# The two mixers of a hybrid block, written out as one sequence per engine

## The chip, the core and the metric

The kernel runs on one core of a Trainium2 chip. The metric is the time on the device in microseconds (us), of which the median of several runs is taken. TensorE (PE) multiplies, VectorE (DVE) and ScalarE (ACT) do elementwise work, GpSimd (POOL) a few small things, and SyncE (SP) starts the loads.

## The reference

The input is 256 tokens of width 1024. A first block (two layers) is followed by a second block (two layers); the change is in the second. `swiglu`, the projections and the norms stay as they are.

```python
for l in range(DEPTH):                                   # DEPTH = 2
    x = x + 0.5 * swiglu(rms_norm_2(x, ffn1_norm[l]), ffn1_gate[l], ffn1_up[l], ffn1_down[l])
    h = rms_norm_2(x, mix_norm[l]) @ w_in[l]
...
    y_pool = pool_mixer(u_pool, pool_w[l], pool_scale[l])        # windows 2, 4, 8, 16
    y_moba = moba_attention(qm, km, vm)                          # 4 heads of 64, causal here
    y_dil = dilated_attention(qd, kd, vd)                        # 4 heads of 64, causal, dilations 1, 4, 16
    y_conv = conv_module(u_conv, conv_w[l], conv_b[l], conv_ln_g[l], conv_ln_b[l])   # 31 taps
    mix = jnp.concatenate([y_pool, y_moba, y_dil, y_conv], axis=-1)
    x = x + mix @ w_out[l]
    x = x + 0.5 * swiglu(rms_norm_2(x, ffn2_norm[l]), ffn2_gate[l], ffn2_up[l], ffn2_down[l])
```

With 256 tokens both attentions are a softmax over a table of added logits (`biasc`), and half of that table, the keys after a query, is masked.

## The kernel before

All weights are cut into chunks of 128 x 2048 numbers (1 MB), which one list puts in order (`plan`, L99). SyncE loads a chunk into one of five slots of `raw` as soon as the chunk five places earlier is used up. ScalarE rounds it to `whi` (L733, four slots), VectorE writes the remainder to `wlo` (L1320): this pair of steps is the split. TensorE then multiplies each chunk in 48 products of 128 x 256 (weights high by activations high, high by low, low by high), all of them recorded on L994, the line of the helper `mm`.

The activations lie feature-major: 128 features on the partitions, 256 tokens along them. In the mixer of one layer there are nine chunks of projections (cg and ca for the convolution, qm, km, qd, kd for the queries and keys, up, vm, vd token-major for the pool and the values) and four output chunks wo. Each projection fills one of four banks `accM`; VectorE or ScalarE takes it out before the bank is used again. Queries and keys are rotated: VectorE scales the product twice (L1544, L1545), TensorE multiplies by a rotation matrix (`rot`), VectorE adds (L1627).

There are eight heads, in the steps `scores` (two products of a 64-row query by key), bias and maximum on VectorE (L1642, L1645), exponent on ScalarE (L914), `turn` (four transposes, L1181), a copy on ScalarE (L920), `mix` (the turned weights by the values, token-major), division by the row sum on VectorE (L1678, L1681), `back` (transposes to feature-major, L1208), and the high and low parts (L940, L1697). The convolution is 31 taps of two instructions on VectorE (L1705, L1707), followed by statistics over features (`cstats`) and a normalisation (`cspread`), whose results are the last quarter of the wo product.

What sets the order: `plan` gives each step a chunk position, and sorts the steps of one position by kind. Each engine goes through the chunks. TensorE spreads the steps of a position evenly over the eight parts of that chunk's product, unless the chunk needs one of them first. VectorE does what it takes out of a finished product, then some steps, then the split of the chunk three ahead, then the others; the taps go in six parts of five or six. Three lines set this:

```python
for n in range(TAP_PARTS):
    at(base + 2 + n, "taps", l, n)
for pos in sorted(todo):
    steps.setdefault(min(pos, base + 12), []).extend(sorted(todo[pos], key=lambda s: order[s[0]]))
```

## Time and profile before

| | us |
|---|---|
| median of 3 runs | 2279.4 |
| lowest, highest | 2274.05, 2287.24 |
| the profiled execution | 2291.71 |
| its span, first to last instruction | 2289.9 |
| TensorE busy | 2166.0 |
| VectorE busy | 1439.4 |
| ScalarE busy | 1006.9 |

The page gives the busy time of each engine; matmuls overlap, so a busy TensorE may still be slow. The stretches tell how many instructions fell into a part of the span and which clock TensorE was granted there (1.00 is full speed). In the chain of waits each step is followed back to what released it, so the distance of two starts is what an instruction costs on the path. In the order of time, a bracket behind a row says how long the engine had been idle and for whom.

### The profile page before, as it was taken

What the parts mean: (1) busy time and instruction counts of PE and PEld (TensorE: products, weight loads), DVE (VectorE), ACT (ScalarE), POOL (GpSimd) and SP (SyncE); (2) the same over time, 40 slices, a digit from 0 to 9 for tenths busy, and PEclk for the clock granted to TensorE, in tenths of its full rate; (3) what the DMA queues carried; (4) which work ended last, traced back from release to release, by engine and by line L of the source; (5) the groups of instructions that cost most, each with busy time, mean ns of one, the idle gap of its engine ahead of it and who ended that gap; (6) DMA issues with size and microseconds to landing.
All of it is one profiled execution on the core that took longest, in us unless ns stands there. A gap on an engine that the chain in (4) does not pass through costs nothing.

```text
span 2289.9 us, 39444 instructions
## 1 busy us (share of the span) xinstructions
PE 2166.0 (95%) x17460; PEld 2108.3 (92%) x17460; DVE 1439.4 (63%) x1701; ACT 1006.9 (44%) x1166; POOL 49.1 (2%) x58
## 2 busy tenths in 40 slices
PE   7999999899899999989997999879999999879998
PEld 7999999899889999989997999769999999769997
DVE  6565564666665556457675756856656656855664
ACT  5554354444455444444444443334444434333442
POOL 1000000000000000000000000000000000000000
PEclk8999999999999999999998999889999999979999
DMA  5444543355344455445552555314555554313552
GB/s 198 163 149 172 182 181 140 137 184 186 134 155 172 150 184 184 148 142 186 189 190 99 184 185 184 111 56 156 196 192 183 181 189 176 129 56 130 185 186 90
DMA packets 52858, 366.08 MB, mean 160 GB/s; under 512 B 5904, under 2 KB 5904, under 8 KB 9296
## 3 DMA queue, kind: packets, MB, share of 16 engines
q1 hardware_dynamic: 52272, 361.21, 43.9%
q8 instruction: 138, 2.26, 0.4%
q0 software_dynamic: 416, 2.35, 0.3%
q14 instruction: 32, 0.26, 0.0%
HBM read 362.49 MB, written 1.05 MB: 159 GB/s over the span
## 4 chain that ended last, share of the span: by engine, by line
PE 75%; DVE 10%; issue 10%; ACT 4%; DMA 1%; POOL 1%; POOLq 0%; ACTq 0%; DVEq 0%
PE accM L994 43%; PE scoreP L994 16%; PE outP L994 8%; PE turnP L994 7%; DVE wlo L1320 3%; DVE yc L1707 1%; ACT whi L733 1%; PE turnP L1181 1%; ACT ew L914 1%; ACT xh L746 1%; PE outP L1208 0%; DMA raw<-in_W 0%; ACT sq L752 0%; DVE cen L1398 0%; DVE cen L1404 0%
## 5 line engine op out<-in xcount | busy, mean ns | idle before, releaser
L1320 DVE TENSOR_TENSOR wlo<-raw,whi 128x2048 fp32r<-128x2048 f32 x336 | 768.5, 2290 | 417.4 <-ACT whi L733 416.1
L733 ACT ACTIVATE whi<-raw 128x2048 fp32r<-128x2048 f32 x336 | 638.5, 1908 | 240.9 <-PE accM L994 139.9
L994 PE MATMUL accM<-xh,whi 128*128 128x256 f32 x1152 | 339.2, 294 | 11.2 <-DVE xl L1418 10.4
L994 PE MATMUL scoreP<-xh,whi 128*128 128x256 f32 x1152 | 328.3, 285 | 13.9 <-DVE xl L1418 9.4
L994 PE MATMUL scoreP<-xl,whi 128*128 128x256 f32 x1152 | 326.2, 283 | 0.0
L994 PE MATMUL scoreP<-xh,wlo 128*128 128x256 f32 x1152 | 326.1, 283 | 0.0
L994 PE MATMUL accM<-xl,whi 128*128 128x256 f32 x1152 | 325.6, 283 | 0.0
L994 PE MATMUL accM<-xh,wlo 128*128 128x256 f32 x1152 | 325.3, 282 | 0.0
L994 PE MATMUL accM<-fh,whi 128*128 128x256 f32 x1056 | 296.8, 281 | 4.1 <-DVE wlo L1320 4.1
L994 PE MATMUL accM<-fl,whi 128*128 128x256 f32 x1056 | 296.5, 281 | 0.0
L994 PE MATMUL accM<-fh,wlo 128*128 128x256 f32 x1056 | 296.5, 281 | 0.0
L994 PEld LDWEIGHTS accM<-xh,whi 128*128 128x128 f32 x1152 | 220.8, 192 | 21.8 <-issue 21.6
L994 PEld LDWEIGHTS scoreP<-xh,whi 128*128 128x128 f32 x1152 | 221.5, 192 | 14.9 <-issue 14.3
L994 PEld LDWEIGHTS accM<-xl,whi 128*128 128x128 f32 x1152 | 220.6, 192 | 2.7 <-issue 2.5
L994 PEld LDWEIGHTS accM<-xh,wlo 128*128 128x128 f32 x1152 | 222.3, 193 | 0.0
L994 PEld LDWEIGHTS scoreP<-xh,wlo 128*128 128x128 f32 x1152 | 221.2, 192 | 0.0
L994 PEld LDWEIGHTS scoreP<-xl,whi 128*128 128x128 f32 x1152 | 220.8, 192 | 0.2
L994 PEld LDWEIGHTS accM<-fh,whi 128*128 128x128 f32 x1056 | 200.0, 189 | 4.8 <-DVE wlo L1320 4.8
L994 PEld LDWEIGHTS accM<-fh,wlo 128*128 128x128 f32 x1056 | 200.0, 189 | 0.0
L994 PEld LDWEIGHTS accM<-fl,whi 128*128 128x128 f32 x1056 | 199.2, 189 | 0.0
L994 PE MATMUL turnP<-xl,whi 128*128 128x256 f32 x480 | 134.5, 280 | 0.0
L994 PE MATMUL turnP<-xh,wlo 128*128 128x256 f32 x480 | 134.5, 280 | 0.0
(263 smaller groups left out, 4256.3 us busy)
## 6 DMA issues: line engine op xcount, KB each, us to landing
raw<-in_W SPq DMA_DIRECT2D x336, 1024.0 KB, 4.8
biasr<-in_bias SPq DMA_DIRECT2D x16, 256.0 KB, 2.7
raw<-in_memT SPq DMA_DIRECT2D x2, 1024.0 KB, 5.4
cc<-in_consts POOLq DMA_DIRECT2D x1, 1536.0 KB, 7.1
x<-in_xT SPq DMA_DIRECT2D x4, 256.0 KB, 4.3
out<-x SPq DMA_DIRECT2D x4, 256.0 KB, 2.5
c<-in_consts SPq DMA_DIRECT2D x1, 464.5 KB, 6.2
par<-in_par POOLq DMA_DIRECT2D x2, 203.5 KB, 3.6
```

The source lines that it names most:

```text
L733: nc.scalar.activation(whi[:, hi_slot(c), :], raw[:, raw_slot(c), :], ACT.Copy).then_inc(split_hi.sem, 1)
L746: ins = nc.scalar.activation(xh[:, k, :], x[:, k, :], ACT.Copy, scale=gain(n, k))
L914: ins = nc.scalar.activation(ew[:, e0 + i, :], src, ACT.Exp, bias=negmax[:, e0 + i:e0 + i + 1], scale=scale, accum_out=rsum[:, s0 + i:s0 + ...
L994: return nc.tensor.matmul(dst, a, b, start=start, stop=stop, skip_group_check=True)
L1181: ins = nc.tensor.transpose(turnP[:, k * S + t * P:k * S + (t + 1) * P], src[t][:, k * P:(k + 1) * P], ident)
L1320: v.tensor_tensor(wlo[:, raw_slot(c), :], raw[:, raw_slot(c), :], whi[:, hi_slot(c), :].bitcast(F32), ALU.subtract).then_inc(split_lo.sem, 1)
L1707: ins = v.scalar_tensor_tensor(yc[:, m, :], src, w, yc[:, m, :], ALU.mult, ALU.add)
```

## The change

The nine projections and four wo chunks no longer take their steps from the plan. For each mixer, every engine now has one written-out function `mixer(l)`, which lists products in eighths, taps one by one, splits and head steps. `product` takes a range of its eight parts (k0, k1). The wo chunks come in the order 1, 0, 2, 3, where it was 0, 1, 3, 2. Banks are named in a table. The norm ahead of the mixer is cut in pieces (`norm_front`, `norm_var`, `norm_diag`), with splits between them.

The heads change in form. Scores, bias, maximum and exponent leave out the block of keys 128 to 255 for queries 0 to 127, which is masked: 384 columns stand where 512 stood. The division by the row sum is done on the exponents before the turn (`even`). `weigh` takes the values as the stationary side, so that the result comes out feature-major in 64 rows, two heads in one bank; `otok` and the `back` transposes go. The order of the other stages is unchanged.

```diff
+MIXER_BANKS = {"cg": "acc0", "ca": "acc1", "qm": "acc2", "qm turned": "acc0", "km": "acc3", "km turned": "acc1",
+               "qd": "acc2", "qd turned": "acc3", "kd": "acc0", "kd turned": "acc1", "up": "acc1", "vm": "acc2",
+               "heads 0": "acc2", "heads 1": "acc1", "vd": "acc0", "heads 2": "out", "heads 3": "out"}
...
-            for r, k in (("cg", "F"), ("ca", "F"), ("qm", "F"), ("km", "F"), ("qd", "F"), ("kd", "F"),
-                         ("up", "T"), ("vm", "T"), ("vd", "T")):
-                c = add(k, r, l)
-                if r in ("qm", "km", "qd", "kd"):
-                    at(c + 2, "rot", chunks[c])
-                if r == "up":
-                    at(c + 2, "pool", chunks[c])
-                    at(c + 2, "poolw", chunks[c])
...
-            for j in (0, 1, 3, 2):
+            for j in (1, 0, 2, 3):
...
-            for n in range(TAP_PARTS):
-                at(base + 2 + n, "taps", l, n)
...
+            def exponent(l, i):
+                act.wait_ge(mix_maxed.sem, mix_maxed.at((l, i)))
+                if i >= 2:
+                    act.wait_ge(mix_turned.sem, mix_turned.at((l, i - 2)))
+                for t in range(2):
+                    e, s0 = 2 * (i % 2) + t, 2 * (i % 4) + t
+                    ins = nc.scalar.activation(ew[:, e, keys(t)], logits(i)[:, tri(t)], ACT.Exp,
+                                               bias=negmax[:, e:e + 1], accum_out=rsum[:, s0:s0 + 1])
+                ins.then_inc(mix_expd.sem, 1)
+
+            def keep_turned(l, i):
+                act.wait_ge(mix_turned.sem, mix_turned.at((l, i)))
+                if i >= 2:
+                    act.wait_ge(mix_weighed.sem, mix_weighed.at((l, i - 2)))
+                nc.scalar.activation(turned_heads(i)[:, 0:TRI], turnP[:, 0:TRI], ACT.Copy)\
+                    .then_inc(mix_turn_kept.sem, 1)
+
+            def heads_hi(l, pair):
+                act.wait_ge(mix_weighed.sem, mix_weighed.at((l, 2 * pair + 1)))
+                nc.scalar.activation(zh[:, 2 + pair, :], mixer_bank(f"heads {pair}")[:, 0:S], ACT.Copy)\
+                    .then_inc(mix_hi.sem, 1)
...
+                move_tokens(m["up"])
+                keep_turned(l, 1)
+                keep_pool(l)
+                pool_hi(l)
+                move_tokens(m["vm"])
+                exponent(l, 2)
+                split_next(m["wo2"])
+                exponent(l, 3)
+                heads_hi(l, 0)
+                keep_turned(l, 2)
...
-            def product(c, hooks):
+            def product(c, hooks, k0=0, k1=KT):
...
+            def rotate(c):
+                l, r = c["l"], c["role"]
+                bank[MIXER_BANKS[r + " turned"]].claim(pe, mix_roped, (l, r))
+                pe.wait_ge(mix_took.sem, mix_took.at((l, r)))
+                mm(mixer_bank(r + " turned"), con("rot2"), rraw[:, (r[0] == "k") * 1, :], True)\
+                    .then_inc(mix_rotated.sem, 1)
...
+            def turn(l, i):
+                turnB.claim(pe, mix_turn_kept, (l, i))
+                pe.wait_ge(mix_evened.sem, mix_evened.at((l, i)))
+                for t in range(2):
+                    for k in range(t + 1):
+                        ins = nc.tensor.transpose(turnP[:, (k + t) * P:(k + t + 1) * P],
+                                                  ew[:, 2 * (i % 2) + t, k * P:(k + 1) * P], ident)
+                ins.then_inc(mix_turned.sem, 1)
+
+            def weigh(l, i):
+                kind, j, pair = kind_of(i), i % 4, i // 2
+                if i % 2 == 0:
+                    bank[MIXER_BANKS[f"heads {pair}"]].claim(pe, mix_lo, (l, pair))
+                pe.wait_ge(mix_turn_kept.sem, mix_turn_kept.at((l, i)))
+                pe.wait_ge(mix_moved.sem, mix_moved.at((l, "v" + kind)))
+                v0 = 64 * j + (S if kind == "d" else 0)
+                o = mixer_bank(f"heads {pair}")[64 * (j % 2):64 * (j % 2) + 64, :]
+                e = turned_heads(i)
+                mm(o[:, 0:S], v2[:, 0, v0:v0 + 64], e[:, 0:S], True, False)
+                mm(o[:, P:S], v2[:, 1, v0:v0 + 64], e[:, S:TRI], False, True).then_inc(mix_weighed.sem, 1)
...
+                product(m["cg"], {})
+                product(m["ca"], {}, 0, 3)
+                norm_stats(n)
+                product(m["ca"], {}, 3, 8)
+                product(m["qm"], {}, 0, 4)
+                norm_spread(n)
+                product(m["qm"], {}, 4, 8)
+                product(m["km"], {}, 0, 3)
+                rotate(m["qm"])
...
+                product(m["vm"], {}, 7, 8)
+                rotate(m["kd"])
+                product(m["vd"], {}, 0, 1)
+                weigh(l, 0)
+                product(m["vd"], {}, 1, 2)
+                weigh(l, 1)
...
+                product(m["wo0"], {}, 5, 8)
+                conv_stats(l)
+                turn(l, 4)
+                turn(l, 5)
+                weigh(l, 4)
+                turn(l, 6)
+                weigh(l, 5)
+                turn(l, 7)
+                weigh(l, 6)
+                weigh(l, 7)
+                conv_spread(l)
+                product(m["wo2"], {})
+                product(m["wo3"], {})
...
+            def root_scaled(c):
+                r = c["role"]
+                dve.wait_ge(used.sem, used.at(c["c"]))
+                cos, sin = (csr[:, i, :].unsqueeze(1).broadcast_to([P, 2, S]) for i in range(2))
+                rr = rraw[:, (r[0] == "k") * 1, :].rearrange("p (m s) -> p m s", m=2)
+                v.tensor_tensor(rr, pair_of(c), sin, ALU.mult)
+                v.tensor_tensor(turned_to(c), pair_of(c), cos, ALU.mult).then_inc(mix_took.sem, 1)
+
+            def rotated_sum(c):
+                l, r = c["l"], c["role"]
+                dve.wait_ge(mix_took.sem, mix_took.at((l, r)))
+                dve.wait_ge(mix_rotated.sem, mix_rotated.at((l, r)))
+                v.tensor_tensor(turned_to(c), mixer_bank(r + " turned").rearrange("p (m s) -> p m s", m=2),
+                                turned_to(c), ALU.add).then_inc(mix_roped.sem, 1)
+
+            def add_bias(l, i):
+                dve.wait_ge(mix_scored.sem, mix_scored.at((l, i)))
+                if i >= 2:
+                    dve.wait_ge(mix_expd.sem, mix_expd.at((l, i - 2)))
+                v.scalar_tensor_tensor(logits(i)[:, 0:TRI], scoreP[:, i % 2, 0:TRI], 0.125,
+                                       biasc[:, (kind_of(i) == "d") * 1, :], ALU.mult, ALU.add)\
+                    .then_inc(mix_biased.sem, 1)
+
+            def maximum(l, i):
+                dve.wait_ge(mix_biased.sem, mix_biased.at((l, i)))
+                for t in range(2):
+                    e = 2 * (i % 2) + t
+                    ins = v.tensor_reduce(negmax[:, e:e + 1], logits(i)[:, tri(t)], AX, ALU.max, negate=True)
+                ins.then_inc(mix_maxed.sem, 1)
+
+            def even(l, i):
+                dve.wait_ge(mix_expd.sem, mix_expd.at((l, i)))
+                s, s0 = mrs[:, 10 + 2 * (i % 2):12 + 2 * (i % 2)], 2 * (i % 4)
+                link(v.reciprocal(s, rsum[:, s0:s0 + 2]))
+                for t in range(2):
+                    e = ew[:, 2 * (i % 2) + t, keys(t)]
+                    ins = v.tensor_scalar(e, e, s[:, t:t + 1], None, ALU.mult)
+                ins.then_inc(mix_evened.sem, 1)
...
+            def heads_lo(l, pair):
+                dve.wait_ge(mix_hi.sem, mix_hi.at((l, pair)))
+                v.tensor_tensor(zl[:, 2 + pair, :], mixer_bank(f"heads {pair}")[:, 0:S],
+                                zh[:, 2 + pair, :].bitcast(F32), ALU.subtract).then_inc(mix_lo.sem, 1)
...
+                split_next(m["qm"])
+                split_next(m["km"])
+                norm_var(n)
+                split_next(m["qd"])
+                norm_diag(n)
+                split_next(m["kd"])
+                keep_spread(n)
+                gate_scaled(m["cg"])
+                scale_tables()
+                root_scaled(m["qm"])
+                conv_scaled(m["ca"])
+                conv_gated(l)
+                split_next(m["up"])
+                taps(l, 0, 1)
+                rotated_sum(m["qm"])
...
+                taps(l, 30, 31)
+                add_bias(l, 6)
+                even(l, 4)
+                add_bias(l, 7)
+                maximum(l, 6)
+                even(l, 5)
+                maximum(l, 7)
+                conv_var(l)
+                even(l, 6)
+                split_next(m["wo2"])
+                even(l, 7)
+                heads_lo(l, 2)
+                conv_diag(l)
+                split_next(m["wo3"])
+                heads_lo(l, 3)
+                split_next(m["sg0"])
+                conv_centre(l)
+                split_next(m["su0"])
+                conv_act(l)
+                conv_lo(l)
```

The order that results, in two places. VectorE in the first mixer, amid the taps, before: yc is the convolution's sum, wlo a split, rraw, q2 and k2 belong to the rotation.

```order
L1320 TENSOR_TENSOR wlo<-raw,whi 128x2048
L1707 SCALAR_TENSOR_TENSOR yc<-hpad,par,yc 128x256 x10
L1544 TENSOR_TENSOR rraw<-accM,angle 128x512
L1545 TENSOR_TENSOR k2<-accM,angle 128x512
L1627 TENSOR_TENSOR q2<-accM,q2 128x512
L1320 TENSOR_TENSOR wlo<-raw,whi 128x2048
L1707 SCALAR_TENSOR_TENSOR yc<-hpad,par,yc 128x256 x10
L1544 TENSOR_TENSOR rraw<-accM,angle 128x512
L1545 TENSOR_TENSOR q2<-accM,angle 128x512
L1627 TENSOR_TENSOR k2<-accM,k2 128x512
```

And after, a little later in the taps: negmax and logit are maximum and bias, ew the exponents.

```order
L1812 SCALAR_TENSOR_TENSOR yc<-hpad,par,yc 128x256 x2
L1845 TENSOR_REDUCE negmax<-logit 128x1 x2
L1812 SCALAR_TENSOR_TENSOR yc<-hpad,par,yc 128x256 x2
L1845 TENSOR_REDUCE negmax<-logit 128x1 x2
L1812 SCALAR_TENSOR_TENSOR yc<-hpad,par,yc 128x256 x2
L1837 SCALAR_TENSOR_TENSOR logit<-scoreP,cc 128x384
L1812 SCALAR_TENSOR_TENSOR yc<-hpad,par,yc 128x256 x2
L1851 RECIPROCAL mrs<-rsum 128x2
L1854 TENSOR_SCALAR ew<-ew,mrs 128x128
L1854 TENSOR_SCALAR ew<-ew,mrs 128x256
L1812 SCALAR_TENSOR_TENSOR yc<-hpad,par,yc 128x256 x2
L1851 RECIPROCAL mrs<-rsum 128x2
```

Five taps in a row became single taps, each followed by one step of a head, of a rotation or by a split.

TensorE where the last heads are done, before: outP takes the convolution's spread, a transpose and a head, and accM the products of a wo chunk.

```order
L994 MATMUL accM<-zh,wlo 128x256
L994 MATMUL accM<-zh,whi 128x256
L994 MATMUL accM<-zl,whi 128x256
L994 MATMUL accM<-zh,wlo 128x256
L994 MATMUL outP<-diag,ones 128x128 x4
L1208 MATMUL outP<-c0,otok 128x128 x2
L994 MATMUL outP<-v2,eT 128x64 x4
L994 MATMUL accM<-zh,whi 128x256
L994 MATMUL accM<-zl,whi 128x256
L994 MATMUL accM<-zh,wlo 128x256
```

And after, behind the chunk wo0:

```order
L1331 MATMUL turnP<-c0,ew 128x128 x6
L1098 MATMUL outP<-eT,v2 64x256
L1098 MATMUL outP<-eT,v2 64x128
L1331 MATMUL turnP<-c0,ew 128x128 x3
L1098 MATMUL outP<-eT,v2 64x256
L1098 MATMUL outP<-eT,v2 64x128
L1331 MATMUL turnP<-c0,ew 128x128 x3
L1098 MATMUL outP<-eT,v2 64x256
L1098 MATMUL outP<-eT,v2 64x128
L1098 MATMUL outP<-eT,v2 64x256
L1098 MATMUL outP<-eT,v2 64x128
L1098 MATMUL outP<-diag,ones 128x128 x4
```

The turns and weighings of the last four heads, which stood a few at a time between parts of wo chunks, now stand in one row, between wo0 and wo2.

## Rows read from the trace of the kernel before

**Rows 1.** the page, busy time by engine: us, share of the span, instructions

```profile
PE 2166.0 (95%) x17460; PEld 2108.3 (92%) x17460; DVE 1439.4 (63%) x1701; ACT 1006.9 (44%) x1166; POOL 49.1 (2%) x58
```

**Rows 2.** busy time by stretch: from:to, length, then busy us (instructions), granted clock, DMA

```profile
1406.00:1563.00 157.00, 131.79 (x918) 119.10 (x918) 106.94 (x185) 56.53 (x92) 1.38 (x2) 0.89 0.28 101
...
1926.00:2083.00 157.00, 130.65 (x895) 118.53 (x894) 104.22 (x179) 54.51 (x88) 1.38 (x2) 0.87 0.28 101
```

**Rows 3.** tile accM on PE, first mixer: ns min/median/max, first and last start

```profile
L994 PE MATMUL accM<-xh,whi x96: 275/277/1202, 1417.6 to 1462.2; 128*128 128x256 f32 x96
...
L994 PE MATMUL accM<-zh,wlo x64: 275/280/416, 1515.7 to 1563.1; 128*128 128x256 f32 x64
```

**Rows 4.** the same for the second mixer

```profile
L994 PE MATMUL accM<-xh,whi x96: 275/281/1202, 1938.2 to 1983.2; 128*128 128x256 f32 x96
...
L994 PE MATMUL accM<-zh,wlo x64: 276/280/416, 2033.7 to 2085.6; 128*128 128x256 f32 x64
```

**Rows 5.** chain of waits, in a feed-forward stage: start, us, work

```profile
1259.48 11.31 PE scoreP L994 x96
```

**Rows 6.** chain of waits inside the first mixer

```profile
1447.27 0.60 DVE q L1545
1447.87 2.20 DVE wlo L1320
...
1500.89 0.44 PE turnP L1181 x4
1501.33 0.71 PE accM L994 x6
...
1503.38 1.06 PE scoreP L994 x4
1504.43 0.90 PE accM L994 x6
...
1552.75 0.84 PE outP L994 x8
```

**Rows 7.** DVE in order of time, first mixer: start, us, line, work

```profile
1449.98 4.55 DVE L1707 SCALAR_TENSOR_TENSOR yc<-hpad,par,yc 128x256 f32<-128x256 f32 x10
...
1512.87 0.42 DVE L1428 TENSOR_TENSOR diag<-outP,c 128x256 f32<-128x256 f32 x1
...
1516.91 0.42 DVE L1697 TENSOR_TENSOR zl<-outP,zh 128x256 fp32r<-128x256 f32 x1
```

**Rows 8.** costliest groups, first mixer, shapes apart: busy us, mean ns, idle before

```profile
L1642 DVE SCALAR_TENSOR_TENSOR logit<-scoreP,cc 128x512 f32<-128x512 f32 x8 | 5.5, 688 | 11.8 <-PE scoreP L994 11.8
L1645 DVE TENSOR_REDUCE negmax<-logit 128x2 f32<-128x512 f32 x8 | 5.5, 686 | 0.3
...
L994 PE MATMUL outP<-cc,up 128*64 128x256 f32 x16 | 2.5, 463 | 0.0
```

**Rows 9.** tile ew on DVE, whole program: ns min/median/max

```profile
L1658 DVE TENSOR_SCALAR ew<-ew,mrs x16: 347/352/356, 53.5 to 696.6; 128x256 f32<-128x256 f32 x16
```

**Rows 10.** PE in order of time, first mixer, two rotations

```profile
1448.02 2.04 PE L994 MATMUL accM<-rraw,c 128*128 128x512 f32 x2 [5.51 <-DVE q L1545]
...
1456.11 1.10 PE L994 MATMUL accM<-rraw,c 128*128 128x512 f32 x2
```

**Rows 11.** DVE in order of time, first mixer, a late head

```profile
1527.08 0.69 DVE L1642 SCALAR_TENSOR_TENSOR logit<-scoreP,cc 128x512 f32<-128x512 f32 x1 [5.05 <-PE scoreP L994]
```

**Rows 12.** three-us stretches of the first mixer, columns as in rows 2

```profile
1448.00:1451.00 3.00, 2.98 (x8) 1.97 (x9) 2.96 (x4) 0.00 (x0) 0.00 (x0) 0.51 0.00 0
...
1484.00:1487.00 3.00, 3.00 (x9) 1.94 (x9) 2.90 (x7) 0.00 (x0) 0.00 (x0) 0.50 0.03 8
...
1514.00:1517.00 3.00, 1.82 (x11) 1.82 (x12) 2.02 (x11) 1.34 (x2) 0.69 (x1) 0.80 0.00 0
...
1541.00:1544.00 3.00, 3.00 (x20) 3.00 (x20) 0.30 (x2) 0.00 (x0) 0.00 (x0) 0.65 0.00 0
...
1547.00:1550.00 3.00, 3.00 (x28) 3.00 (x27) 0.42 (x1) 1.54 (x3) 0.00 (x0) 1.00 0.13 22
```

More of the change, by code:

```diff
@@ L812, in take @@
                 if "ends" in c:
+                    if c["role"] == "sd" and c["f"] == 0:
+                        norm(c["ends"])
+                        return True
                     norm(c["ends"], lambda: split_at(pos + 2),
@@ L1248, in _ @@
+            PE_STEPS = ("rot", "back", "mix", "turn", "scores")
             SPREAD = 8
@@ L1305, in _ @@
             v = nc.vector
-            BEFORE_SPLIT = ("scores", "rot", "back",
-                            "mix", "turn", "yc", "lam", "cstats", "cspread", "pool", "poolw")
+            BEFORE_SPLIT = ("scores", "rot", "back", "mix", "turn", "yc", "lam")
             def split(c):
@@ new lines, in taps @@
+            def taps(l, i0, i1):
+                for i in range(i0, i1):
+                    for m in range(2):
+                        src, w = tap(i, m)
+                        if i == 0:
+                            ins = v.tensor_scalar(yc[:, m, :], src, w, col("conv_b", m, 1, P2), ALU.mult, ALU.add)
+                        else:
+                            ins = v.scalar_tensor_tensor(yc[:, m, :], src, w, yc[:, m, :], ALU.mult, ALU.add)
+                    if i < TAPS - 1:
+                        link(ins)
+                    else:
+                        ins.then_inc(tapped.sem, 1)
```

627 lines of the change are left out of this document (399 added, 228 removed).

## The prediction

> **What bounds the kernel now.** I read the page first: TensorE is busy 2166 of 2289.9 us [rows 1], so outside its gaps nothing but matmul work sets the time. Then the stretches: the two in which the mixers lie have the low granted clocks, 0.89 and 0.87, and only 918 and 895 matmuls in 157 us [rows 2], where a feed-forward stage puts 96 products into 11.31 us [rows 5]. A chunk of 48 matmuls therefore costs 5.65 us, 0.118 us each. The change touches the two mixers alone, so everything else stays.
>
> A mixer begins with the first product of chunk cg and ends with the last product of the last wo chunk. The first runs from 1417.6 to 1563.2 [rows 3], the second from 1938.2 to 2085.7 [rows 4]: 145.6 and 147.5 us, mean 146.5. Its 13 chunks are 13 x 5.65 = 73.5 us of TensorE. So some 73 us of each mixer are head steps, waits and half clock. Three views say which. TensorE waits 5.51 us for VectorE, which is still in its taps when qm's product needs scaling [rows 10]. VectorE waits in turn for TensorE's scores, 11.8 us in sum, 5.05 us once at the end [rows 8, 11]. And behind each longer gap stands a granted clock of 0.50, the lower of the two levels (1.2 GHz against 2.4) [rows 12]: the rotation that waited took 2.04 us and the later one, at full clock, 1.10 [rows 10]. Engines take turns here; none is busy throughout (VectorE 107 of 157 us).
>
> **VectorE in the changed mixer.** The order is now one list, so I sum it. Distances from start to start in the chain of waits are what an instruction costs in a row: a split 2.20 us, an operation over 512 columns 0.60 [rows 6]. Ten tap instructions take 4.55 us, so one tap (two instructions) 0.915 with its hand-over [rows 7].
> - 13 splits (qm to su0): 28.6.
> - 31 taps: 28.4, as before, only cut finer; each piece already waits for its own chain.
> - 20 operations of 512 columns (gate, tables, four times two scalings and a sum, two for the convolution's input, four at its end): 12.2.
> - Bias: 384 columns where 512 cost 688 ns [rows 8]. Between 0.60 in a row and 0.42, what 256 columns take [rows 7], I take 0.50; eight: 4.0.
> - Maximum: one instruction of 686 ns [rows 8] becomes two of 128 and 256 columns. Bounds 0.42 (one of 256) and 0.84; I take 0.62; eight: 5.0.
> - Normalising now before the turn: a reciprocal and two scalings of ew, 128 and 256 columns; 256 cost 0.352 in the same form [rows 9]. I take 0.80 (bounds 0.55 and 0.95); eight: 6.4. The old normalisation, on 64 columns twice, goes.
> - Statistics, diagonals, low parts: the convolution's are 4.0 us from 1512.87 to 1516.91, with a 0.8 us visit to GpSimd that the new order covers [rows 7]; with the norm's and the five small ones 7.3.
>
> Together 92 us, against 107 of busy time in the old window, which holds other stages too [rows 2]. The first split starts 7.2 us after cg, as today (the norm before it is unchanged).
>
> **TensorE in the changed mixer.** 13 chunks, 73.5. Scores: 1.06 for 512 columns [rows 6]; 384 bring 0.80, and I add 0.15 because the six products behind scores took 0.90 and not 0.71 [rows 6]: eight, 7.6. Turns: three transposes where four took 0.44 [rows 6]: with the return 0.5, eight, 4.0. Weighing: today's mix is 0.84 for four products per tile pair [rows 6]. The new one streams 384 columns onto 64 output rows; scaled from the scores that is 0.80. Bounds 0.64 and 1.06; I take 0.95 with the return: 7.6. The four `back` transposes go, and with them VectorE's way through otok; I count nothing for them, only their waits. Rotations 4 x 1.05 = 4.2. Pool 2.5 [rows 8]; its second half and the statistics, unchanged, about 6.6. Sum 106 us. So both engines are nearly full, and the mixer cannot be shorter than about 106.
>
> At one place a rule speaks against the change. After scores on 64 rows, products come back 0.19 us late (0.90 for 0.71), after transposes they do not [rows 6]. The Trainium skill's page TensorEngine Tiling (Key Properties) says that changing the tiling mode drains TensorE, and by that rule the new weighing, on 64 columns, pays at both of its ends where today's mix on 128 pays nothing: 16 x 0.19 = 3.0 us a mixer, 1.8 more than the 8 x 0.15 in my sum.
>
> **Do they fit together?** I walk both lists with these durations, t counted from cg's first product. Five VectorE splits and the norm go ahead of the first tap, which starts at t = 22. TensorE has only 1 us of gap by then: the norm's statistics sit inside ca, the spread inside qm, and qm is scaled (t = 20) before km ends (t = 26), so the 5.51 us gap is gone. The banks are free each time (qd in acc2 at 26, kd in acc0 at 33). TensorE ends kd at 42, vm at 59.5. Here VectorE waits: exponent(2) stands on ScalarE behind `keep_pool`, `pool_hi` and `move_tokens(vm)`, and ends at about 61.5, where VectorE wants it at 59 for even(2): 2.6 us. heads_lo(1) waits for vd's last head, 2.0. The convolution's statistics cost 0.8 (TensorE ends wo0 at 86 and the statistics at 88), small ones 0.6. So VectorE ends at 7.2 + 92 + 6 = 105.5 with conv_lo. wo2 starts at 98, behind heads_lo(3), and ends at 104; wo3 needs conv_lo, so the mixer ends at 105.5 + 5.65 = 111 us. What is late last is VectorE's list, no longer a round trip.
>
> **The clock.** I add 2 us. Between t = 86 and 98 TensorE has some 7 us of small steps in 12; at 1514 such a stretch fell to 0.80 [rows 12]. If wo2 starts at half clock it costs at most 5 us more, of which the wait for conv_lo covers 2. The Trainium skill (TensorE: Matmul & The Clock Gate, "Why this matters for your kernels") advises against idle gaps between bursts, as the clock drops after them; by that rule the old gaps of 5.51 us would be throttled, and the trace agrees [rows 10, 12].
>
> Hence 113.5 us a mixer against 146.5: 33 saved each, 66 in both. The profiled execution took 2291.7 us (span 2289.9 and 1.8 around it) and gives 2225.7; it was 12.3 above the median of the runs shown, and nothing in the mixers makes that difference, so from the median 2279.4 I come to **2213.4 us**.
>
> **Rivals.**
> - A, the forecast: the lists mesh, mixers of 107 to 119 us, as the small terms go to their bounds; savings of 55 to 79 us give 2200 to 2224. Chance 0.64.
> - B, the clock stays low for longer: the list puts 16 small fp32 steps with waits into vm and vd, where half clock lasted from about 1484 [rows 12]. Each 10 us of TensorE's full-clock work done at half clock is 10 us more, since TensorE has only 5 us of slack; one or two such pieces give mixers of 119 to 132, 2224 to 2250. For it: the clock falls after gaps. Against: by the walk no gap above 2.6 us is left. Chance 0.17.
> - C, nearly no waits: TensorE's own 106 us and smaller steps, mixers of 100 to 107, 2186 to 2200. Against it: three waits that I can name. Chance 0.10.
> - D, an interlock: strict lists let no engine go past a late step, so a single step put too early (rotate(kd), weigh(2) or exponent(2)) holds a whole list, 8 to 12 us, each mixer. Two such holds give 2250 to 2270. Chance 0.04.
> - E, slower: half clock through the head stage and the tail. TensorE's 106 us would need 146.5 - 111 = 35 us of them at half clock just to lose the gain, a third of its work; at half of the work (53 us) a mixer takes 164 and the kernel 2314. For it: the old mixer had twelve of these 3-us stretches, 36 us, at 0.66 or less, the first at 1448 and the last at 1541 [rows 12]. Against: those followed gaps that the new order closes. Chance 0.05, 0.02 of it within the bound of no change.
>
> **How the numbers follow.** The likeliest case gives 2213. The range must leave out 2 in 10 at most: from 2194 (all of A and 0.04 of C's 0.10) to 2243 (0.13 of B's 0.17), which holds 0.81. A measurement of this kernel can tell 0.5%, 11 us, from no change: faster by more is A, B, C and D, 0.95; within 0.5% 0.02; slower 0.03.
>
> **What would show it.** Right: from cg's first product to wo3's last some 113 us in both mixers; granted clock over that stretch above 0.95; VectorE over 90% busy from the first tap to conv_lo; wo3's first product released by the low part of the convolution (zl, 512 columns). Wrong: a gap of TensorE over 3 us before vd; stretches at 0.50 during vm, vd or wo1; a weighing step over 1.1 us at full clock; ScalarE's exponents waited for by more than 3 us. Each mixer at 125 us would mean B, and stretches outside the mixers that differ by over 5 us would mean that I overlooked an edit.

## The result

The changed kernel takes 2202.4 us (median of 4 runs, 2196.8 to 2202.7) where the kernel before took 2278.0 on the same chip (4 runs, 2274.1 to 2287.2): ratio 0.966, 95% interval 0.962 to 0.969, 75.6 us less. The forecast was 2213.4 in a range of 2194 to 2243. The mixers' part came out larger than forecast, and one sentence of the reasoning does not hold for most of the mixer: which engine is late.

The changed kernel's page, busy time by engine as in [rows 1]:

```profile
PE 2117.2 (96%) x17364; PEld 2059.8 (94%) x17364; DVE 1432.3 (65%) x1717; ACT 1003.6 (46%) x1166; POOL 53.1 (2%) x58
```

TensorE's busy time fell by 48.8 us with 96 instructions fewer; 33.8 of that lie in the two mixers, and the last section says where the rest may come from. VectorE's and ScalarE's hardly moved, so the gain is not work taken off those two. A mixer is read from the first product of cg to the last of the last wo chunk. For the first one (tile accM on PE: ns min/median/max, first and last start), as in [rows 3]:

```profile
L1098 PE MATMUL accM<-xh,whi x96: 276/281/682, 1403.8 to 1445.4; 128*128 128x256 f32 x96
...
L1098 PE MATMUL accM<-zh,wlo x64: 276/279/280, 1474.5 to 1512.5; 128*128 128x256 f32 x64
```

And the busy times of just those two stretches (columns as in [rows 2]), first of the kernel before, then of the changed one:

```profile
1417.60:1563.10 145.50, 120.29 (x821) 107.60 (x820) 98.44 (x173) 51.27 (x85) 1.38 (x2) 0.88 0.26 95
1938.20:2085.60 147.40, 121.87 (x820) 109.93 (x821) 97.58 (x172) 50.27 (x82) 1.38 (x2) 0.86 0.26 93
```

```profile
1403.80:1512.60 108.80, 102.81 (x774) 91.44 (x773) 95.21 (x182) 49.78 (x86) 3.35 (x2) 1.00 0.35 127
1886.80:1997.00 110.20, 105.53 (x774) 93.23 (x773) 95.40 (x182) 49.83 (x86) 3.35 (x2) 0.95 0.34 125
```

146.5 us became 109.5, 37.0 in each mixer. The account for the first: TensorE stood for 25.2 us (145.5 - 120.3) and stands for 6.0. Of its 120.3 busy us some 13.5 were the extra time of the half clock: in each 3-us stretch the busy time times one minus the granted clock, summed over the mixer. At full clock its work was 106.8 us and is 102.8. So 36.7 = 19.2 less standing + 13.5 less half clock + 4.0 less work. This is a book of where the time lay; what caused what is the experiments' matter.

The two mixers give 74.0 and the medians 75.6, which agree. The two profiled executions differ by 89.0 (2291.71 and 2202.72): the first mixer began 13.8 us earlier in the changed kernel's, ahead of any changed instruction. The last section says what that is.

TensorE's waits in the first mixer of the changed kernel (engine, what it was to do, line, for whom: us in all, times, longest):

```profile
PE turnP L1331 <- ACT eT L1015: 2.2, 2, 1.5
PE outP L1098 <- DVE zl L1859: 1.8, 1, 1.8
PE accM L1098 <- DVE zl L1895: 1.0, 1, 1.0
PE turnP L1331 <- DVE ew L1854: 0.7, 1, 0.7
```

All of them lie behind 1489.2, in the last fifth of the mixer. Until then TensorE has no gap above 0.2 us in 85 us. In the second mixer, and in both of the control below, it has one more, of 0.7 us, for the norm's diagonals at t = 16 (t counts from the mixer's first product). The 5.51 us ahead of the rotation [rows 10] and the 5.05 us for which VectorE waited on a late head's scores [rows 11] are gone.

### The profile page after: what moved, and what is told of

It is laid out like the page before. It is cut to its first block, busy times and chain, and to the rows that moved or that the text cites. A ratio compares the mean times of both kernels' runs of the same rounds, so it can differ in the third digit from the quotient of the medians.

```text
span 2200.9 us, 39332 instructions
## 1 busy us (share of the span) xinstructions
PE 2117.2 (96%) x17364; PEld 2059.8 (94%) x17364; DVE 1432.3 (65%) x1717; ACT 1003.6 (46%) x1166; POOL 53.1 (2%) x58
## 4 chain that ended last, share of the span: by engine, by line
PE 80%; issue 9%; DVE 7%; ACT 3%; POOL 1%; DMA 0%; POOLq 0%; ACTq 0%; DVEq 0%
PE accM L1098 48%; PE scoreP L1098 16%; PE outP L1098 7%; PE turnP L1098 7%; DVE wlo L1531 2%; ACT whi L747 1%; PE turnP L1278 1%; ACT xh L765 1%; ACT ew L926 1%; ACT x L812 0%; POOL small L689 0%; PE outP L1304 0%; ACT sq L771 0%; DVE cen L1625 0%; DVE mrs L2064 0%
## 5 line engine op out<-in xcount | busy, mean ns | idle before, releaser
L1098 PE MATMUL turnP<-xh,whi 128*128 128x256 f32 x480 | 133.4, 278 | 0.0
```

The source lines that it names most:

```text
L1098: return nc.tensor.matmul(dst, a, b, start=start, stop=stop, skip_group_check=True)
```

## The experiments

Twelve kernels, each timed in five rounds beside the kernel before, whose median was 2274.1, 2274.7 and 2275.0 in the three sessions. "Mixers" is read in each profile as above. The changed kernel itself, run once more (control_after), is what the others are compared with; it ran in the first session only, so the eight kernels of the later two are compared across chips. Its profile has both mixers undisturbed, that is without half clock:

| kernel | median us | ratio to before, 95% | mixers us | each against control |
|---|---|---|---|---|
| control_after | 2201.4 | 0.969, 0.966 to 0.972 | 108.8, 108.7 | |
| taps_in_six | 2218.7 | 0.977, 0.973 to 0.981 | 118.2, 118.0 | +9.4 |
| six_taps_moved | 2212.6 | 0.973, 0.970 to 0.977 | 111.5, 113.9 | +4.0 |
| full_squares | 2208.2 | 0.972, 0.968 to 0.975 | 112.1, 112.4 | +3.5 |
| load_in_body | 2221.1 | 0.976, 0.973 to 0.979 | 118.0, 117.5 | +9.0 |
| load_body_filled | 2211.2 | 0.973, 0.969 to 0.976 | 112.9, 112.8 | +4.1 |
| load_in_tail | 2215.0 | 0.974, 0.971 to 0.977 | 114.5, 114.6 | +5.8 |
| load_at_waits | 2202.3 | 0.970, 0.967 to 0.973 | 109.1, 109.3 | +0.5 |
| tail_reordered | 2193.8 | 0.966, 0.963 to 0.969 | 106.8, 106.7 | -2.0 |
| square_first | 2194.4 | 0.964, 0.960 to 0.967 | 105.3, 105.1 | -3.6 |
| before_filled | 2269.8 | 0.998, 0.996 to 1.001 | 141.8, 143.8 | (-3.7 against before) |
| before_taps_later | 2285.0 | 1.006, 1.003 to 1.008 | 148.0, 149.8 | (+2.5 against before) |

The medians carry some 5 us of scatter from other stages, so a difference of a few us is read from the mixers of one profile of each kernel, and where both speak they agree in sign. A difference under about 1 us in a mixer is not told from nothing: TensorE's busy time on the same work differs by that much between undisturbed mixers (101.9 to 102.9 us).

> The changed kernel once more, unaltered, beside the three that follow, so that all four are compared on one chip. Both theories expect 2202 us or near it, and mixers of 109 to 110 us.

It repeats: 2201.4 against 2202.4, mixers of 108.8 and 108.7.

**Which part of the change paid: the placing of the taps.** The 31 taps go back into six blocks:

```diff
-                taps(l, 24, 25)
-                pool_lo(l)
-                taps(l, 25, 26)
+                pool_lo(l)
+                taps(l, 25, 31)
                 split_next(m["wo0"])
...
```

> The changed kernel, but with VectorE's 31 taps gathered again into six runs (0-4, 5-9, 10-14, 15-19, 20-24, 25-30), each where its first tap stands now; nothing else is moved. Theory (the order makes the gain, since TensorE no longer waits for VectorE's taps): VectorE reaches its second scaling 2.7 us later, where TensorE has 0.4 us of slack today, and the later runs hold scores and maxima back too; 2 to 6 us more per mixer, with half clock behind the gaps perhaps, so 2206 to 2216 us. Rival (only the projections' start matters, the cut taps do nothing): within 2 us of the control. Second rival (the cut of the taps is the whole gain): mixers of 130 us and more, over 2240 us.

It cost 9.4 us a mixer, more than the 2 to 6 expected. VectorE in order of time, where it hurts (start, us, line, work, idle before and its releaser):

```profile
1474.95 5.45 DVE L1812 SCALAR_TENSOR_TENSOR yc<-hpad,par,yc 128x256 f32<-128x256 f32 x12
1480.32 2.28 DVE L1531 TENSOR_TENSOR wlo<-raw,whi 128x2048 fp32r<-128x2048 f32 x1
...
1491.36 0.56 DVE L1837 SCALAR_TENSOR_TENSOR logit<-scoreP,cc 128x384 f32<-128x384 f32 x1 [4.22 <-PE scoreP L1098]
```

The block of six taps holds up the split of wo0. TensorE runs dry for 2.42 us at 1482.65, works at a granted clock of 0.50 behind it, and VectorE then pays 4.22 us waiting for scores that come late. By the sum used above, the half clock's extra time is 6.6 of the 9.4 us in either mixer, and TensorE stands only 2.9 us longer than in the control, so more of the loss is booked on the clock than on the waits. The next kernel moves that one block behind the maximum of group 5 and changes nothing else:

```diff
-                taps(l, 25, 31)
                 split_next(m["wo0"])
                 add_bias(l, 4)
                 maximum(l, 4)
                 add_bias(l, 5)
                 maximum(l, 5)
+                taps(l, 25, 31)
```

> The version with the taps in six blocks (which was 17 us slower than the changed kernel), with its last block of six taps moved from ahead of the split of wo0 to behind the maximum of score group 5. Same instructions, same six blocks. Theory: what that version lost was one place, the split and the scores of the late heads that waited 5.3 us behind the block while TensorE stood (gaps of 2.4 and a half clock behind them); 3 to 6 us of the 9.3 in each mixer come back, 6 to 12 in all. Rival: it lost by the number of blocks, each of which holds something up a little: under 2 in each mixer comes back. A second rival: the stats of the local branch come later by the block and eat all that is won: no gain or a loss.

5.4 of the 9.4 come back: one place made more than half of the loss. 2.2 of the rest is TensorE's wait for the scaled k, which VectorE does behind the first block of five taps (rotated sum of qm, then the scaling of km), a row in both profiles:

```profile
PE accM L1098 <- DVE k L1824: 2.2, 1, 2.2
```

The second mixer lost 2.4 more than the first, and only there did half clock follow (13.6 us of its stretches). TensorE's wait for k was 2.2 us in both, so a gap of this length may or may not bring the half clock.

**The triangular scores.** Scores, bias, exponents and turns over full squares again (bias 512 columns, four turns, weighing 256 columns each):

```diff
-TRI = P + S
+TRI = 2 * S
...
-                    for k in range(t + 1):
+                    for k in range(2):
```

> The changed kernel with the masked block of keys put back into the heads: scores, bias, maximum, exponent, scaling and turn over 512 columns, four transposes, two products of 256 columns in the weighing; the order is unaltered. Theory (the form of the heads is a small part): TensorE does about 4 us more per mixer and VectorE about 4, both full, so 4 to 6 us per mixer and 2210 to 2215 us. Rival (the smaller heads make the gain): 15 us or more per mixer, over 2232 us.

3.5 us a mixer, a little under the 4 to 6 expected and far from the rival's 15. TensorE's busy time in the first mixer is 105.3 against 102.2, 3.1 us more. VectorE's is longer too, by 2.7 us (bias 1.1, maximum 1.1, scaling of the exponents 0.5). Both engines got nearly the same amount of extra work, so this run prices the triangle but does not say which of them binds.

**Who binds where.** The prediction says that VectorE's list is late last, the trace says that TensorE has no gap until 1489. Seven useless operations of 512 columns go into VectorE's list at two places:

```diff
                 taps(l, 3, 4)
+                load(7)
...
                 conv_diag(l)
+                load(7)
```

> The changed kernel with seven more operations in VectorE's list behind the fourth tap (otok = cs2 * csr, 128x512, each 0.69 us and by the step from start to start 0.61, so 4.3 us in each mixer; nothing reads the result). Theory: until the stats of the local branch TensorE has no gap, it is TensorE's own sum that binds there, and VectorE's waits for others in that stretch (0.6 + 1.2 + 2.2 = 4.0 us in the profile) take the 4.3 in: 0 to 2 us in each mixer, 0 to 4 in all. Rival (what the prediction's text says, that VectorE's list binds all through the mixer): 4 us or more in each, 8 to 10 in all.

> The changed kernel with the same seven operations (4.3 us in each mixer) behind the diagonal of the local branch's stats, that is in the tail. Theory: there VectorE's list is what everything waits for, nothing hides them: 4 to 5 us in each mixer, 8 to 10 in all. Rival: TensorE's sum binds to the end, the tail has slack too: under 2 in each.

The load was larger than reckoned: 5.05 us in the rows, 0.72 each with the hand-over, where 4.3 stood in the expectations. The tail paid all of it, 5.8 us; the 0.7 on top came with some 7 us at half clock in each mixer, most of them inside TensorE's wait. The body missed both expectations: 9.0 us a mixer, nearly twice the load, where 0 to 2 was the theory and 4 or more, 8 to 10 in both mixers together, the rival. Three-us stretches of that kernel's first mixer:

```profile
1434.00:1437.00 3.00, 3.00 (x28) 3.00 (x27) 2.96 (x4) 0.00 (x0) 0.00 (x0) 1.00 0.18 76
1437.00:1440.00 3.00, 1.33 (x12) 1.13 (x10) 2.86 (x5) 1.92 (x1) 0.00 (x0) 1.00 0.64 208
1440.00:1443.00 3.00, 0.41 (x2) 0.44 (x3) 2.90 (x6) 0.00 (x0) 0.00 (x0) 0.55 0.34 142
1443.00:1446.00 3.00, 3.00 (x11) 2.13 (x11) 2.93 (x7) 0.00 (x0) 0.00 (x0) 0.50 0.02 5
1446.00:1449.00 3.00, 3.00 (x11) 2.35 (x11) 2.97 (x4) 0.00 (x0) 0.00 (x0) 0.50 0.00 0
...
1452.00:1455.00 3.00, 3.00 (x25) 2.81 (x24) 2.06 (x6) 0.47 (x1) 0.00 (x0) 1.00 0.00 0
```

```profile
PE scoreP L1098 <- DVE k L1830: 4.3, 1, 4.3
```

The load stands ahead of the rotated sum of km, and TensorE wants k for the first scores just when it is done. So TensorE stood for 4.3 us, and then did 11 matmuls in 3 us where it does 22 to 28 at full clock, until about 1451. My theory read "no gap" as "slack", which it is not. The next kernel divides the 9.0. It fills the gap with idle products, so that only the clock differs:

```diff
                 product(m["kd"], {}, 0, 2)
+                pe.wait_ge(outB.reader[0].sem, outB.reader[0].at(outB.reader[1]))
+                for _ in range(8):
+                    mm(outP[:, 0:S], ones[:, :], con("cos1"), True)
                 scores(l, 0)
```

> The version with seven more VectorE operations behind the fourth tap (which made each mixer 9.0 us longer, for 5.05 us of operations), with eight products of ones by a table of cosines (full float32, 256 columns, some 0.5 us each, 4.1 us in all, result read by nobody) on TensorE ahead of the first scores, where it stood for 4.3 us. Theory: the 9.0 us were 4.3 of standing and then 9 to 12 us in which the same work ran at a granted clock of 0.50; with the gap filled the clock stays, and 3 to 4.5 us in each mixer come back, 6 to 9 in all. Rival: the 9.0 come from the chain of VectorE and ScalarE that the load shifts, whatever the clock: 0 to 1 in each.

```profile
1441.00:1444.00 3.00, 3.00 (x22) 2.82 (x22) 2.86 (x5) 1.92 (x1) 0.00 (x0) 1.00 0.60 169
1444.00:1447.00 3.00, 2.19 (x11) 1.64 (x10) 2.90 (x5) 0.00 (x0) 0.00 (x0) 1.00 0.44 186
1447.00:1450.00 3.00, 3.00 (x18) 2.20 (x19) 2.93 (x7) 0.00 (x0) 0.00 (x0) 1.00 0.00 0
```

With the gap filled the granted clock stays at 1.00 and 4.9 of the 9.0 are gone, a little more than expected, in both mixers nearly alike (5.1 and 4.7). The same VectorE load costs 4.1 without the half clock and 9.0 with it. (In the first mixer of load_in_body the clock fell a second time, in the tail at 1500 to 1510; in the second only behind the gap.) Another kernel puts five such operations where VectorE itself waits:

```diff
+                load(2)
                 even(l, 2)
...
+                load(3)
                 heads_lo(l, 1)
```

> The changed kernel with the same kind of VectorE operations where VectorE itself waits for ScalarE: two ahead of the normalising of head 2 (wait there 1.2 us) and three ahead of the split of head pair 1 (wait 2.2 us); 0.72 us each, 3.6 us in each mixer. Theory (VectorE has slack at these waits and none at the place of the earlier load): 0 to 1 us in each mixer, 0 to 2 in all. Rival (what the prediction says, VectorE's list is what is late all through): 3.6 in each, 7 in all.

```profile
1462.14 1.42 DVE L1999 TENSOR_TENSOR otok<-cs,angle 128x512 f32<-128x512 f32 x2
1463.59 0.17 DVE L1851 RECIPROCAL mrs<-rsum 128x2 f32<-128x2 f32 x1
...
1471.01 2.14 DVE L1999 TENSOR_TENSOR otok<-cs,angle 128x512 f32<-128x512 f32 x3
1473.19 0.42 DVE L1859 TENSOR_TENSOR zl<-accM,zh 128x256 fp32r<-128x256 f32 x1
```

3.6 us of load cost 0.5 us a mixer: both waits (1.19 and 2.17 us in the changed kernel) have vanished from the rows and the load stands in their stead. TensorE's busy time on the same work is 0.5 to 1.0 us above the control's, so the 0.5 may be no cost at all. VectorE's list is thus not late without a break: it has slack of 1 to 2 us at two places in the body, some 0.7 at the rotated sum of km (5.05 of load made a wait of 4.3), and none in the tail. This refutes the rival as it stood, but it is less than a test of the prediction, whose walk had waits of VectorE at just these two places (2.6 and 2.0 us). That TensorE sets the pace of the body rests on its having no gap there. The chain of waits of the changed kernel says the same: it stays on TensorE from the start of the first mixer and passes to VectorE only here (start, us, work):

```profile
1487.63 1.74 PE outP L1098 x8
...
1489.40 0.43 DVE diag L1655
```

**How much of the old loss was the clock.** The same filling in the kernel before, in five of its gaps (n is 10, 4, 6, 3 and 6 products, put in ahead of the step that waits):

```diff
+                for _ in range(n):
+                    mm((outP if to == "out" else turnP)[:, 0:S], ones[:, :], con("cos1"), True)
...
+                fill(name, what)
```

> The kernel before with idle products on TensorE (as above, 256 columns, 0.5 us at full clock) in its gaps, so that the clock has less reason to fall: 10 ahead of the rotation of qm, 4 ahead of qd's, 6 ahead of the turn of head 1, 3 ahead of the local branch's stats and 6 ahead of its spread. Everything else, the order on VectorE too, is as before. In the profile of before TensorE is busy 120.8 us of the first mixer and the mean granted clock there is 0.88, that is some 35 us of 146 at the half clock. Theory A (the waits set the time, the half clock only works inside them): 0 to 3 us less in each mixer. Theory B (the half clock is a price of its own, as the 9.0 us for a load of 5.05 suggest): 5 to 12 us less in each, 10 to 24 in all, and the granted clock of the mixers rises to 0.95 or more.

```profile
1402.30:1544.10 141.80, 124.40 (x879) 112.21 (x878) 98.43 (x174) 51.13 (x84) 1.38 (x2) 0.96 0.28 97
1919.10:2062.90 143.80, 127.35 (x878) 115.45 (x879) 97.54 (x172) 50.20 (x83) 1.38 (x2) 0.94 0.27 96
```

3.7 us a mixer, just above theory A's 3 and below B's 5. By the same sum as above the half clock's extra time fell from 13.5 to 4.2 us in the first mixer, so 9.3 us of clock were won and only 3.7 of time. The other 5.6 or so turned into longer standing, for the engines it waited for were no faster: standing and idle products together are 30.9 us (17.4 + 13.5) where standing was 25.2. In the kernel before, the clock's fall lay mostly inside the waits. In the changed one it depends on the place. In the body it counts nearly in full: by the same sum 4.8 us of half clock in the second mixer of load_in_body, and 4.7 us of time. In the tail, where TensorE waits anyway, a part is covered: 4.2 us in the second mixer of the changed kernel, and 1.4 us of time. The medians (5.1 us, interval of the ratio up to 1.0005) can't prove this gain; the mixers of one profile carry it.

**A part alone in the kernel before.** Each of the six blocks of taps (not three, as the expectation has it), and the square, the stats and the spread behind them, one chunk later:

```diff
-                at(base + 2 + n, "taps", l, n)
-            at(base + 2 + TAP_PARTS, "csquare", l)
-            at(base + 9, "cstats", l)
-            at(base + 10, "cspread", l)
+                at(base + 3 + n, "taps", l, n)
+            at(base + 3 + TAP_PARTS, "csquare", l)
+            at(base + 10, "cstats", l)
+            at(base + 11, "cspread", l)
```

> The kernel before with each of its three blocks of taps, and the square, the stats and the spread of the local branch, one chunk later: one part of the change alone, and in the coarse steps of the kernel before. Theory (one gap closed leaves the others; the block only changes whom it holds up): the 5.5 us gap at the rotation of qm goes or shrinks, and each mixer gains 0 to 5 us, 0 to 10 in all, of the 37 in each that the whole change gave. Rival (the place of the taps is most of what was lost): 10 us or more in each.

Both theories missed, since it is 2.5 us a mixer slower. The gap of 5.51 us ahead of the rotation [rows 10] is gone (the longest such wait in the first mixer is 1.7 now), and two others grew in its stead, from 3.69 and 3.82 us at the same steps (the first mixer again):

```profile
1497.70 1.97 PE L994 MATMUL outP<-v,eT 128*128 128x64 f32 x8 [7.30 <-DVE zl L1697]
...
1535.53 0.66 PE L1208 MATMUL outP<-c,otok 128*128 128x128 f32 x2 [5.45 <-DVE zl L1730]
```

TensorE stands for 30.5 us in that mixer, where it stood for 25.2. The wait of 7.30 is behind a block: VectorE does six taps in one piece (5.46 us from 1491.86) just ahead of the low part that TensorE needs. The wait of 5.45 is behind the spread and its bank, which this edit moved too, so the run does not price the blocks alone. At the two places tried in this kernel, blocks in one piece held somebody up. The cut into pieces that fit between two steps somebody waits for is worth some 9 us of the 37, by taps_in_six; that is its price with everything else of the change in place.

**A better order.** The changed kernel's waits of TensorE lie in the tail, all but the 0.7. This version puts scores and the convolution's stats into wo1 and wo0 earlier, deals wo0's products out between the turns, gives the spread a bank of the scores in place of the heads' bank, covers three waits of VectorE, and moves the split of su0 behind the low part of the convolution:

```diff
-                product(m["wo0"], {}, 5, 8)
+                product(m["wo0"], {}, 0, 3)
                 conv_stats(l)
                 turn(l, 4)
+                product(m["wo0"], {}, 3, 4)
                 turn(l, 5)
+                product(m["wo0"], {}, 4, 6)
                 weigh(l, 4)
...
```

> The changed kernel with its ends meshed anew. TensorE is full up to the end of wo0 there, VectorE from then on. So: scores of the last two heads move into wo1, the convolution's statistics in front of wo0's last five eighths, which then fill the gaps between the last turns and weighings; the convolution's spread goes to a bank of scoreP, so that it doesn't wait for the low part of the last heads; on VectorE three waits are covered (the bias of head 2, the scaling of head 2 and the low part of the second pair each move behind other work) and the split of su0 moves behind the convolution's low part; on ScalarE the exponents 4 and 5 go ahead of a split that waits for wo1. Theory (TensorE is short of its 5.9 us of gaps only at the tail, VectorE has 5 us of waits before it): 3 to 5 us less per mixer, 2192 to 2197 us, TensorE's gaps per mixer under 3 us. Rival (the chain turn, copy, weigh, high part, low part of the last heads binds by its own latency): less than 1 us per mixer, 2200 to 2203 us.

2.0 us a mixer, less than the 3 to 5 expected, and TensorE still stands for 4.7 us and not under 3. Its two longest waits name what is left:

```profile
PE accM L1098 <- DVE zl L1862: 1.5, 1, 1.5
PE outP L1098 <- ACT yc L973: 1.3, 1, 1.3
```

The 1.3 is the stats' wait for the square, which stands on ScalarE behind a split that nobody needs yet:

```diff
-                split_next(m["sg0"])
                 conv_square(l)
+                split_next(m["sg0"])
```

> The version with the reordered tail, and in ScalarE's list the square of the convolution ahead of the split of sg0 in place of behind it. In the profile of the reordered tail TensorE waits 1.3 us for this square, which stands behind a split of 1.8 us. Theory (the tail is one chain and each of its waits counts): 1 to 1.3 us in each mixer, 2 to 3 in all, against the reordered tail. Rival: another chain (the late heads' turns, through ScalarE) ends as late: 0 to 0.5 in each.

1.6 us a mixer more, where 1 to 1.3 was expected, and the row of 1.3 is gone. Together 3.6 us a mixer, 7 in all: 2194 us against 2201. That is 0.3%, less than the medians can tell apart; both mixers of both profiles show it.

## Why the prediction was right, and where it was not

- **What goes.** The round trips and the 5.51 us gap went, as said. The forecast of a mixer was 113.5 us, it took 109.5; 66 saved in both were forecast, 74 measured. Of the 4.0, some 2.4 are VectorE's sum and 1.3 the clock, both below, and 0.3 is a slip: 7.2 + 92 + 6 is 105.2 and not 105.5.
- **The signs named beforehand.** The granted clock was 1.00 and 0.95. VectorE was busy for 71.4 of the 78.2 us from the first tap to conv_lo, 91%. There was no gap of TensorE above 0.7 us before the tail, no stretch at 0.50 before t = 87, no weighing above 0.86 us at full clock, and no wait for exponents above 1.2. These came true.
- **"What is late last is VectorE's list": wrong for four fifths of the mixer.** TensorE has no gap but the 0.7 to t = 85, and load_at_waits shows VectorE with slack on the way. It is right for the tail: wo3's first product is released by the convolution's low part (zl L1895, wait 1.0 to 1.2) in the first mixer and in both of the control, and load_in_tail costs its whole length. The walk had all this in it, both engines near full and VectorE waiting twice. The sentence summed it up wrongly. The forecast did not suffer, as the two engines' sums (106 and 105 us) were so close that either one as the binding engine gives nearly the same time; to that extent the right number is luck and no proof of the sentence.
- **VectorE's sum.** 92 us plus 6 of waits behind a start at 7.2 gave conv_lo at 105.5, and wo3's first product came at t = 103.1. Mis-sized terms: normalising 0.67 for 0.80 (-1.0 in eight), maximum 0.53 for 0.62 (-0.7), the wait for exponent(2) 1.19 for 2.6 (-1.4). Bias 0.48 for 0.50 and the other waits (2.17 for 2.0, 0.74 for 0.8) were right. These three took 3.1 us off and wo3 came 2.4 earlier, so other terms were some 0.7 too small. Rows of the bias and of a normalisation:

```profile
1439.66 0.56 DVE L1837 SCALAR_TENSOR_TENSOR logit<-scoreP,cc 128x384 f32<-128x384 f32 x1
1440.14 0.87 DVE L1812 SCALAR_TENSOR_TENSOR yc<-hpad,par,yc 128x256 f32<-128x256 f32 x2
...
1464.14 0.17 DVE L1851 RECIPROCAL mrs<-rsum 128x2 f32<-128x2 f32 x1 [1.19 <-ACT ew L1007]
1464.35 0.55 DVE L1854 TENSOR_SCALAR ew<-ew,mrs 128x128 f32<-128x128 f32 x2
```

- **TensorE's sum.** 106 us forecast, 102.8 measured at full clock. The terms are costs in the chain of waits with the return to products, so they are read there:

```profile
1437.70 0.85 PE scoreP L1098 x4
1438.55 0.90 PE accM L1098 x6
...
1456.85 1.93 PE outP L1098 x16
...
1468.29 3.07 PE accM L1098 x22
1471.36 0.33 PE turnP L1331 x3
```

A turn of three cost 0.33 for 0.50 (1.4 us in eight) and the pool 1.93 for 2.5 (the row it came from [rows 8] held half clock). Scores cost 0.85 and 0.19 more in the six products behind them, 1.04 for 0.95, which goes the other way by 0.7. Weighing was sized right: the 22 matmuls from 1468.29 are 18 products, 2.12 us at 0.118, and one weighing, which leaves 0.95. The rest of the 3.2 I did not find in single terms.
- **The drain on a change of tiling** (the Trainium skill, TensorEngine Tiling, Key Properties) would have put 1.8 us more into the sum, and the sum was too large without it. The trace of the changed kernel has its price. A weighing and the product behind it:

```profile
1463.79 0.86 PE L1098 MATMUL accM<-eT,v 128*64 128x256 f32 x4
1464.59 0.38 PE L1098 MATMUL accM<-whi,xh 128*128 128x256 f32 x1
```

From start to start a weighing takes 0.80 us, and 0.95 with its return, so the changes of tiling at its two ends cost at most some 0.15 together, less than half of the 0.38 (0.19 at each end) that I priced by the rule. A turn changes no tiling and has 0.08 of the same kind (0.33 against 0.25 from start to start), so how much of the 0.15 is the drain stays open.
- **The clock.** 2 us a mixer were forecast, in the stretch between the late heads and wo2. It fell just there, in the second mixer alone (1976 to 1988) and in neither of the control's, 1.4 us in one mixer of four, although the waits are alike in all four. A three-us stretch of that mixer:

```profile
1979.00:1982.00 3.00, 2.69 (x11) 1.35 (x10) 2.67 (x7) 0.92 (x3) 0.00 (x0) 0.50 0.00 0
```

- **Rival B's price** was right for the body and too high for the tail. It says that TensorE's work at half clock is paid in full once TensorE binds. Load_in_body against load_body_filled shows it in the body (second mixer: 4.7 us of time for 4.8 of half clock). In the tail the second mixer of the changed kernel paid 1.4 for 4.2.
- **Rival D**, an interlock by one step too early or too late, did not happen. Load_in_body and taps_in_six are what it would look like, 9 us a mixer each. Its range is a slip: two holds of 8 to 12 us in each mixer give 2245 to 2261, not 2250 to 2270.
- **"Stretches outside the mixers that differ by over 5 us would mean that I overlooked an edit": wrong as a test.** They differed by 14 us with no edit there. Between the mixers it was 374.2 and 375.0 us, but ahead of them the cadence of the products differed, which is below.

Two shares are measured, each by taking it out of the changed kernel: 9 us for cutting the taps and 3.5 for the triangle. If they add up, the other 24 us of the 37 are the rest of the change as a whole: strict lists, the order of the wo chunks, the norm in pieces and the feature-major heads. No run parts these, so which of them closed the gaps is argued from the trace and not shown.

## What to carry over

An engine without a gap in the trace is the one that binds there, but the engine feeding it can still be on time by a hair. So measure slack by putting a known load into its list at the place in question; at a place where it waits already, the load only fills the wait. Cut a long run of small operations into pieces that fit between the steps others wait for. While it stays in blocks, the place decides: moving one block gave back 5.4 us of 9.4, moving all six by a chunk cost 2.5. And price a gap of TensorE at its length only where something else is late anyway. Where TensorE binds, the half clock behind a gap can cost about the gap once more (4.7 to 5.1 us behind 4.3), but it does not follow each gap: behind waits of 2.2 us it came in one mixer of six_taps_moved and not in the other.

## What the hardware showed unasked

**Two cadences at the full clock.** The same dense products run at either of two speeds, at a granted clock of 1.00 throughout and with no gap. The changed kernel, 100 us of two feed-forward stages, columns as above:

```profile
440.00:540.00 100.00, 100.00 (x885) 100.00 (x884) 72.14 (x74) 49.71 (x45) 0.00 (x0) 1.00 0.55 194
1270.00:1370.00 100.00, 100.00 (x852) 100.00 (x851) 62.78 (x49) 44.42 (x33) 0.00 (x0) 1.00 0.52 189
```

885 or 852 matmuls in 100 us, nothing between. In its chain of waits (start, us, work) the same 96 products read:

```profile
447.79 10.88 PE scoreP L1098 x96
...
1279.58 11.31 PE scoreP L1098 x96
```

10.88 or 11.31 us, 4% apart ([rows 5] is the slower one, for the kernel before). Over three such stretches in all 14 profiles (440 to 540, 1040 to 1140, 1270 to 1370) 22 were fast and 20 slow, with no tie to the kernel: in the first the kernel before and the control are slow and the changed kernel fast, with the same code there. The products of the feed-forward stage at 440 span 163.6 us in the kernel before and 157.4 in the changed one. Two such stages, those of the first and the second stretch, were fast in the changed kernel's profile and slow in that of the kernel before, which is some 12 of the 13.8 us ahead of the first mixer. It is likely much of the 10 us to either side by which runs scatter. What chooses the cadence stays open; no run varied it.

**Idle products hold the clock.** Thirteen and a half us of products nobody reads, in five gaps, raised a mixer's mean granted clock from 0.88 to 0.96 (from 0.86 to 0.94 in the second), and 3.6 us of them behind one wait kept load_body_filled at 1.00.
